# Final normalisation of the last block: three tiles' products moved from VectorE to ScalarE and GpSimd, the last tile worked in halves

## The chip, the cores and the metric

One core of a Trainium2 chip runs the whole program. The metric is the device time of one execution in microseconds (us), the median of several runs. TensorE multiplies matrices, VectorE (DVE), ScalarE (ACT) and GpSimd (POOL) work element by element, SyncE (SP) issues the transfers. The engines run their own instruction streams in the written order and meet only at semaphores.

## The reference

One step of a decoder layer over 1024 prompt rows and 64 sampled rows of 1024 columns: a matrix memory and a windowed attention, merged and projected, then an MLP with squared ReLU, and at the end a root-mean-square norm with learned weights. The change touches only that norm:

```python
def rmsnorm(x, g):
    y = x * lax.rsqrt(jnp.mean(x * x, axis=-1, keepdims=True) + EPS)
    return y * g

x = x + jnp.square(jax.nn.relu(xn2 @ w_up)) @ w_down
y_prompt, y_sample = rmsnorm(x_prompt_rows, norm_final), rmsnorm(x_sample_rows, norm_final)
```

## The kernel before

The 1088 rows are nine tiles of up to 128 rows (the ninth, tile 8, holds the 64 sampled rows), kept in `x2` in on-chip memory. The MLP's 4096 hidden columns are taken in 16 blocks of 256. Blocks 0 to 14 use a fast matrix scheme with seven half-size products; the last block is done plainly, tile by tile, in the order `DN_ORDER` = 8, 0, 4, 1, 5, 2, 6, 3, 7. Below, n is the place in that order (0 to 8) and not the tile's number, and d = 2n or 2n + 1 is a half tile of 512 columns.

For each half tile TensorE (`last_down`, L1362, products at L1385) makes a sum in one of six PSUM banks, used in turn: half tile d can start when half tile d - 6 has been read. VectorE (`accumulate`, L2390) adds the bank to `x2`. For n = 0 two parts of the sampled rows are first folded together (`fold`, L2396) after a small transfer inside the chip (L839).

Then comes the norm of each tile. ScalarE squares a tile and sums each row (`square`, L1428). GpSimd turns the sum into a rate per row, `rms`: a scaled addition (L2460), then a power of -1/2 (L2462), into `rstd`. VectorE multiplies the tile by rate and weights in one instruction (`normalise`, L1860; for the last tile two instructions of half a tile, L2422) into `ybuf`. SP stores `ybuf` to HBM (L843; the last tile in halves, L847).

`ybuf` has two slots, n % 2. A writer of a slot first waits until the store of tile n - 2 has landed (`y_out`). The weights `gain_b` are loaded at L837, once that buffer is no longer needed by the blocks before.

VectorE's written order is: accumulate 0, 1, 2, fold, final 0, then accumulate 3, final 1, final 2, accumulate 4, final 3, accumulate 5, final 4 and so on to accumulate 8, final 7, final 8. ScalarE's order is the nine squares, GpSimd's the nine rates, SP's the stores by n. Each waits for its inputs' semaphores, and nothing passes what stands ahead of it in its own stream.

Of the kernel before, what the change touches and what calls it, by code (L numbers as in the profile page):

```python
# [32 lines left out]
ALU = mybir.AluOpType  # L33
ACT = mybir.ActivationFunctionType

P = 128
D = 1024
# [4 lines left out]
NT = (T + P - 1) // P  # L42
# [10 lines left out]
EPS = 1e-6  # L53
# [20 lines left out]
def rows_of(i):  # L74
    return P if i < NT - 1 else T - P * (NT - 1)
# [36 lines left out]
MASKW = WIN + (2 * NSEQ - 1) * DSEQ  # L112
UP_UNITS = 2 * len(CHUNKS)
LAST_UNITS = 2 * NT
DN_ORDER = [NT - 1, 0, 4, 1, 5, 2, 6, 3, 7]
NS = NSEQ * DSEQ
FIRST_ORDER = [(0, 0), (0, 1), (0, 2), (1, 1), (1, 2), (1, 0)]
# [4 lines left out]
LAST = NG - 1  # L122
# [12 lines left out]
def up_unit_of(g, u):  # L135

    return (FIRST_ORDER if isinstance(g, int) and g == 0 else UP_ORDER)[u]


def unit_bank(g, u):  # L140

    return (0, 1, 2, 3, 6, 7)[u] if isinstance(g, int) and g == 0 else (6, 7, 0, 1, 2, 3)[u]
# [19 lines left out]
def tile_of(t):  # L162

    return t % NT if t < 2 * NT else DN_ORDER[t % NT]

# [87 lines left out]
def layer_kernel(nc, x_prompt, x_sample, state_C, state_n, state_m, cache_k, cache_v, norm_attn, w_in, b_gate,  # L253
# [9 lines left out]
    def y_rows(i):  # L263
        return y_prompt[0, i * P:(i + 1) * P, :] if i < NT - 1 else ys_flat
# [9 lines left out]
    with ctx:  # L274
# [7 lines left out]
        def sem(name):  # L282
            return ctx.enter_context(nc.semaphore(name))
# [9 lines left out]
        gain_b = sb("gain_b", [P, D])  # L293
# [6 lines left out]
        stat = sb("stat", [P, 3, NT])  # L300
        rstd = sb("rstd", [P, 3, NT])
        neghalf = sb("neghalf", [P, 2])
# [4 lines left out]
        with ExitStack() as s:  # L307
            a = scope_alloc(s)
            x2 = a("x2", [P, NT, D])
# [9 lines left out]
            with ExitStack() as s2:  # L319
                a2 = scope_alloc(s2)  # L320
                ybuf = a2("ybuf", [P, 2, D])
                junk2 = a2("junk2", [P, D])
# [92 lines left out]
        gain_in = sem("gain_in")  # L415
        const_in = sem("const_in")
        consts = sem("consts")
        norm_sq = sem("norm_sq")
        norm_rs = sem("norm_rs")
# [7 lines left out]
        free_v = sem("free_v")  # L427
# [91 lines left out]
        y_out = [sem(f"y_out{n}") for n in range(2)]  # L519
        folded = sem("folded")  # L520
        folded_in = sem("folded_in")
        y_rdy = sem("y_rdy")
        out_dma = sem("out_dma")


# [66 lines left out]
        def read(g, n):  # L592

            return g * DN_READS + (OUT_UNITS + n)
# [12 lines left out]
        def _(sp):  # L607
# [231 lines left out]
            sp.dma_start(hf[0:NS, 0, 0:D], x2[NS:P, NT - 1, :]).then_inc(folded, 16)  # L839
            *sooner, i = DN_ORDER  # L840
            for n, t in enumerate(sooner):
                sp.wait_ge(y_rdy, n + 1)
                sp.dma_start(y_rows(t), ybuf[0:rows_of(t), n % 2, :]).then_inc(y_out[n % 2], 16)  # L843
            for half in range(2):
                at = slice(half * 512, half * 512 + 512)
                sp.wait_ge(y_rdy, NT + half)
                sp.dma_start(y_rows(i)[:, at], ybuf[:, (NT - 1) % 2, at]).then_inc(y_out[(NT - 1) % 2], 16)  # L847
            sp.wait_ge(pc_out, 64)
            sp.wait_ge(cin_out[0], 2 * 16 * PAIRS)
# [6 lines left out]
        def _(pe):  # L856
# [505 lines left out]
            def last_down():  # L1362
# [3 lines left out]
                pe.wait_ge(lo_done, g * UP_UNITS + 4)  # L1366
                for n, i in enumerate(DN_ORDER):
                    if n == 1:
# [39 lines left out]
        def _(act):  # L1408
# [15 lines left out]
            def square(t, src, to):  # L1424
                rows = rows_of(tile_of(t))
                if t:
                    act.wait_ge(norm_sq, t)
                ins = nc.scalar.activation(to[0:rows, :], src, ACT.Square,  # L1428
                                           accum_out=stat[0:rows, t // NT, t % NT:t % NT + 1])
                ins.then_inc(norm_sq, 1)  # L1430
# [318 lines left out]
            for i in range(NT):  # L1749
                t = NT + i  # L1750
# [8 lines left out]
            def split_hid(g, u):  # L1759

                tile, parts, m = hid_parts(g, u)
                c0 = CHUNKS[up_unit_of(g, u)[1]][0]
                for to, at, n in parts:
                    ins = nc.scalar.activation(a_hi[:, to:to + n], relu[:, u % 2, at - c0:at - c0 + n], ACT.Square)
                if m:
                    ins = nc.scalar.activation(smp[:, tile, 0:m], relu[:, u % 2, SEQ - c0:SEQ - c0 + m], ACT.Square)
                ins.then_inc(hi_done, 1)
# [6 lines left out]
            def read_up(g):  # L1774

                sums = not isinstance(g, int) or g < LAST
                for u in range(UP_UNITS):
                    cn = CHUNKS[up_unit_of(g, u)[1]][1]
                    act.wait_ge(gemm_a, g * UP_UNITS + (PROJ_UNITS + u + 1))
                    if u >= 2 or not isinstance(g, int) or g:  # L1780
                        act.wait_ge(lo_done, g * UP_UNITS + (u - 1))
                    nc.scalar.activation(relu[:, u % 2, 0:cn], bank[unit_bank(g, u)][:, 0:cn],  # L1782
                                         ACT.Relu).then_inc(free_a, 1)
                    act.wait_ge(free_a, g * UP_UNITS + (PROJ_UNITS + u + 1))
                    split_hid(g, u)
                    if u == 1:
                        split_mlp(g * 16 + (RAW_ALL[1] + 16), 1)
                    if u == 2 and sums:
                        act.wait_ge(t_f, g * 4 + 4)
                        nc.scalar.activation(t_hi[:, :], tf[:, :], ACT.Copy).then_inc(t_h, 1)  # L1790
                    if u == (3 if not isinstance(g, int) or g else 4) and sums:
                        round_sum(g, S1)
                    if u == 4 and sums:
                        round_sum(g, S2)
                        round_sum(g, S3)
# [26 lines left out]
            with act.Fori(1, LAST) as g:  # L1822
                read_up(g)
                read_down(g)
            read_up(LAST)
            for n, i in enumerate(DN_ORDER):
                if i == NT - 1:
                    act.wait_ge(folded_in, 1)
                else:
                    act.wait_ge(free_v, read(LAST, 2 * n + 2))  # L1830
                square(2 * NT + n, x2[0:rows_of(i), i, :], junk2)

        @block.vector
        def _(dve):
# [345 lines left out]
            at = part_cols(0, 0)  # L2180
# [4 lines left out]
            at = part_cols(0, 1)  # L2185
# [44 lines left out]
            for cq in range(4):  # L2230
                for i in range(NT):
# [9 lines left out]
                    v = x2[0:r, i, cq // 2 * 512:cq // 2 * 512 + 512]  # L2241
                    ins = nc.vector.tensor_tensor(v, bank[m % out_ring(m)][0:r, :], v, ALU.add)
                    if i == NT - 1:
                        link(ins)
                        ins = nc.vector.tensor_tensor(v, bank[m % out_ring(m)][NS:P, :], v, ALU.add)
# [136 lines left out]
            def accumulate(n):  # L2382
                i = DN_ORDER[n]
                for half in range(2):
                    d = 2 * n + half
                    dve.wait_ge(gemm_v, LAST * DN_UNITS + OUT_UNITS + d + 1)
                    v = half_of(i, half)
                    if i < HB:
                        dve.wait_ge(halves, HB * half + i + 1)
                    nc.vector.tensor_tensor(v, bank[LAST_BANKS[d % len(LAST_BANKS)]][:, :], v, ALU.add).then_inc(free_v, 1)  # L2390
# [18 lines left out]
            def final(n):  # L2409
                i = DN_ORDER[n]  # L2410

                def slot():
                    if n >= 2:
                        dve.wait_ge(y_out[n % 2], 16 * (n // 2))
                if n < NT - 1:
                    normalise(2 * NT + n, x2[0:rows_of(i), i, :], ybuf, slot).then_inc(y_rdy, 1)
                    return
                dve.wait_ge(norm_rs, 3 * NT)
                slot()
                for half in range(2):  # L2420
                    at = slice(half * 512, half * 512 + 512)
                    nc.vector.scalar_tensor_tensor(ybuf[:, n % 2, at], x2[:, i, at], rstd[:, 2, n:n + 1], gain_b[:, at],  # L2422
                                                   ALU.mult, ALU.mult).then_inc(y_rdy, 1)

            accumulate(0)
            accumulate(1)
            accumulate(2)
            fold()
            for n in range(2, NT):
                if n > 2:  # L2430
                    accumulate(n)
                if n <= 3:
                    final(n - 2)
                if n >= 3:
                    final(n - 1)
            final(NT - 1)

# [1 line left out]
        def _(pool):  # L2439
            chain = [0]  # L2440

            def link(ins):

                chain[0] += 1
                ins.then_inc(pool_chain, 1)
                pool.wait_ge(pool_chain, chain[0])
# [9 lines left out]
            def rms(t):  # L2456
                rows = rows_of(tile_of(t))
                pool.wait_ge(norm_sq, t + 1)
                v = rstd[0:rows, t // NT, t % NT:t % NT + 1]
                link(nc.gpsimd.tensor_scalar(v, stat[0:rows, t // NT, t % NT:t % NT + 1], 1.0 / D, EPS,  # L2460
                                             ALU.mult, ALU.add))
                nc.gpsimd.tensor_tensor(v, v, neghalf[0:rows, 0:1], ALU.pow).then_inc(norm_rs, 1)  # L2462
# [140 lines left out]
            for q in range(HB):  # L2603
                v = x2[:, q, 0:HD2]
# [3 lines left out]
            for q in range(HB):  # L2608
                lo = x2[:, q, HD2:D]
                nc.gpsimd.tensor_tensor(lo, lo, e6[:, q, :], ALU.add).then_inc(halves, 1)  # L2610
            for t in range(2 * NT, 3 * NT):
                rms(t)


_INS = ["x_prompt", "x_sample", "state_C", "state_n", "state_m", "cache_k", "cache_v", "norm_attn", "w_in", "b_gate",
# [23 lines left out]
```

## Time and profile before

| | us |
|---|---|
| median of 3 runs (lowest, highest) | 1666.8 (1664.81, 1667.55) |
| the profiled execution | 1666.46 |
| its span, first to last instruction | 1664.7 |
| TensorE busy in the span | 1638.7 (98%) |
| VectorE busy | 949.5 (57%) |
| ScalarE busy | 633.2 (38%) |
| GpSimd busy | 349.5 (21%) |

The span is that of the profiled execution; its device time has 1.76 us more around it. The mean granted TensorE clock over the span was 0.996 of full speed. Over the whole span TensorE is the busy engine; the change lies in the last 30 us, from about 1634 us on. TensorE's last product starts at 1654.17 us.

### The profile page before, as it was taken

The numbers are of one execution on the slowest core, as the hardware profiler recorded it, in microseconds if no ns is written. First come the engines' busy times: TensorE is split into PE (matmuls) and PEld (weight loads), VectorE is DVE, ScalarE is ACT, GpSimd is POOL, SyncE is SP. The second block draws the span as 40 slices with busy tenths as digits, with TensorE's granted clock in tenths as the row PEclk, the third lists the DMA queues.
The fourth block names the chain that finished last, engine by engine and source line by source line (L and its number), as shares of the span: only waits on it lengthen the run. The fifth ranks groups of instructions, "written<-read, shape, count | busy, mean of one in ns | idle before, by whom it ended". The sixth has DMA issues, their size and how long they took to land.

```text
span 1664.7 us, 26791 instructions
## 1 busy us (share of the span) xinstructions
PE 1638.7 (98%) x10035; PEld 1496.3 (90%) x10035; DVE 949.5 (57%) x1753; ACT 633.2 (38%) x1407; POOL 349.5 (21%) x351
## 2 busy tenths in 40 slices
PE   8999999999999999999999999999999999999997
PEld 8999899899998899888988899999999999999996
DVE  5413333343145445774545877667777777767787
ACT  5523333232235423553402533433344443343332
POOL 2002001110002100111001233333333222333354
PEclk9999999999999999999999999999999999999999
DMA  7105355352311132311241101111111111111113
GB/s 219 53 26 137 61 73 100 51 88 29 69 29 27 28 82 46 61 27 26 64 134 50 48 29 51 50 50 50 50 33 43 50 50 50 50 38 38 50 63 114
DMA packets 138793, 99.46 MB, mean 60 GB/s; under 512 B 82376, under 2 KB 128464, under 8 KB 138712
## 3 DMA queue, kind: packets, MB, share of 16 engines
q1 hardware_dynamic: 138712, 98.34, 23.8%
q8 instruction: 55, 0.90, 0.2%
q14 instruction: 26, 0.21, 0.0%
HBM read 88.43 MB, written 11.60 MB: 60 GB/s over the span
## 4 chain that ended last, share of the span: by engine, by line
PE 96%; DVE 2%; ACT 1%; issue 1%; DMA 1%; another core or an unknown queue 0%; SPq 0%; POOL 0%; DVEq 0%; POOLq 0%; ACTq 0%
PE bank L911 37%; PE bank L1276 23%; PE bank L1309 6%; PE bank L1310 6%; PE bank L1308 6%; PE bank L1256 5%; PE bank L858 3%; PE bank L1317 2%; PE bank L1097 2%; PE bank L1067 1%; PE bank L976 1%; PE bank L968 1%; PE bank L971 1%; PE bank L1014 1%; PE bank L951 0%
## 5 line engine op out<-in xcount | busy, mean ns | idle before, releaser
L1276 PE MATMUL bank<-xT_hi,w_hi 128*128 128x384 f32 (+1 forms) x768 | 250.7, 326 | 1.0 <-DVE xT_lo L1875 1.0
L1276 PE MATMUL bank<-xT_hi,w_lo 128*128 128x384 f32 (+1 forms) x768 | 250.6, 326 | 0.0
L1276 PE MATMUL bank<-xT_lo,w_hi 128*128 128x384 f32 (+1 forms) x768 | 250.5, 326 | 0.0
L911 PE MATMUL bank<-xT_hi,w_hi 128*128 128x384 f32 (+1 forms) x1008 | 193.9, 334 | 0.0
L911 PE MATMUL bank<-xT_hi,w_lo 128*128 128x384 f32 (+1 forms) x1008 | 186.2, 326 | 0.0
L911 PE MATMUL bank<-xT_lo,w_hi 128*128 128x384 f32 (+1 forms) x1008 | 186.1, 326 | 0.0
L2578 POOL TENSOR_TENSOR e<-gain_b,e 128x512 f32<-128x512 f32 x60 | 78.2, 1304 | 435.0 <-ACT gain_b L1804 435.0
L911 PEld LDWEIGHTS bank<-xT_hi,w_hi 128*128 128x128 f32 x1008 | 166.7, 188 | 2.7 <-issue 1.3
L911 PEld LDWEIGHTS bank<-xT_lo,w_hi 128*128 128x128 f32 x1008 | 168.7, 188 | 0.0
L911 PEld LDWEIGHTS bank<-xT_hi,w_lo 128*128 128x128 f32 x1008 | 168.7, 188 | 0.0
L2358 DVE TENSOR_TENSOR x<-bank,x 128x512 f32<-128x512 f32 x210 | 142.0, 690 | 31.5 <-PE bank L1310 30.9
L1850 DVE TENSOR_TENSOR w_lo<-raw,w_hi 128x1024 fp32r<-128x1024 f32 (+1 forms) x54 | 70.4, 1303 | 155.8 <-ACT w_hi L1421 155.8
L1276 PEld LDWEIGHTS bank<-xT_hi,w_hi 128*128 128x128 f32 x768 | 144.1, 188 | 1.8 <-DVE xT_lo L1875 1.2
L1276 PEld LDWEIGHTS bank<-xT_lo,w_hi 128*128 128x128 f32 x768 | 144.2, 188 | 0.6
L1276 PEld LDWEIGHTS bank<-xT_hi,w_lo 128*128 128x128 f32 x768 | 144.1, 188 | 0.0
L1804 ACT ACTIVATE gain_b<-bank 128x512 f32<-128x512 f32 x120 | 71.8, 599 | 147.2 <-PE bank L1310 82.7
L2298 DVE TENSOR_TENSOR hf<-relu 128x384 f32<-128x384 f32 (+1 forms) x96 | 55.8, 582 | 114.2 <-ACT relu L1782 114.1
L1782 ACT ACTIVATE relu<-bank 128x384 f32<-128x384 f32 (+1 forms) x96 | 45.2, 471 | 197.8 <-PE bank L1276 195.9
L1500 ACT ACTIVATE sig<-bank 128x384 f32<-128x384 f32 (+1 forms) x72 | 34.1, 474 | 173.8 <-PE bank L911 173.8
L1308 PE MATMUL bank<-t_hi,a_hi 128*128 128x512 f32 x240 | 93.4, 389 | 1.3 <-issue 1.3
L1309 PE MATMUL bank<-t_hi,a_lo 128*128 128x512 f32 x240 | 94.2, 393 | 0.0
L1310 PE MATMUL bank<-t_lo,a_hi 128*128 128x512 f32 x240 | 94.1, 392 | 0.0
(275 smaller groups left out, 3009.5 us busy)
## 6 DMA issues: line engine op xcount, KB each, us to landing
raw<-in_w_in SPq DMA_DIRECT2D x64, 256.0 KB, 4.5
raw<-in_w_up SPq DMA_DIRECT2D x16, 1024.0 KB, 5.3
raw<-in_w_down SPq DMA_DIRECT2D x16, 1024.0 KB, 5.0
raw<-in_w_in SPq DMA_DIRECT2D x9, 1024.0 KB, 5.6
xin<-in_x_prompt SPq DMA_DIRECT2D x8, 512.0 KB, 4.0
bc<-gate_rows SPq DMA_DIRECT2D x32, 128.0 KB, 5.7
Cin<-in_state_C SPq DMA_DIRECT2D x4, 1024.0 KB, 8.1
out<-Cin SPq DMA_DIRECT2D x16, 256.0 KB
```

The lines of the kernel that those rows point to most:

```text
L858: return nc.tensor.transpose(out, in_, ident[0:rows, 0:rows])
L911: last = nc.tensor.matmul(out, lhsT, rhs, start=(step == 0), stop=(step == 3 * KT - 1))
L1256: last = nc.tensor.matmul(bank[m % out_ring(m)][0:rows_of(i), :], lhsT, w[:, b % 2, g * 512:(g + 1) * 512], start=(step == 0), stop=(step ...
L1276: last = nc.tensor.matmul(bank[unit_bank(g, u)][:, 0:cn], w[:, 0, k * WCOLS + tile * P:k * WCOLS + (tile + 1) * P], x[:, k, c0:c0 + cn], s ...
L1308: nc.tensor.matmul(out[:, :], a_tile(a_hi, a, q), b_part(b, False), start=True, stop=False)
L1309: nc.tensor.matmul(out[:, :], a_tile(a_lo, a, q), b_part(b, False), start=False, stop=False)
L1310: nc.tensor.matmul(out[:, :], a_tile(a_hi, a, q), b_part(b, True), start=False, stop=True).then_inc(gemm_v, 1)
L1804: nc.scalar.activation(gain_b[:, at:at + HD2], bank[PLACE.index(name) % BANKS][:, :], ACT.Copy).then_inc(free_c, 1)
L1850: ins = nc.vector.tensor_tensor(w_lo[:, b % 2, at], raw[:, b % 2, at], w_hi[:, b % 2, at].bitcast(F32), ALU.subtract)
L2298: nc.vector.tensor_tensor(hf[:, tile, c0:c0 + cn], relu[:, u % 2, 0:cn], relu[:, u % 2, 0:cn], ALU.mult).then_inc(sq_done, 1)
L2358: nc.vector.tensor_tensor(v, src, v, ALU.add).then_inc(free_v, 1)
L2578: nc.gpsimd.tensor_tensor(v, gain_b[:, at:at + HD2], v, ALU.add).then_inc(c_added, 1)
```

## The change

At three places of the order, n = 1, 3, 5 (`Y_POOL`), the final product is no longer one VectorE instruction. ScalarE scales the tile by its row rates into `ybuf` (`scale_row`, in ScalarE's stream behind the square of n + 1, and behind the wait for the slot), and GpSimd multiplies that slot in place by the weights (`scaled_by_gain`, in GpSimd's stream behind the rate of n + 1). SP waits for GpSimd's semaphore `y_pool` for these tiles; its order of stores stays.

For the last tile, ScalarE squares each half of 512 columns as soon as that half is accumulated, into two sums; GpSimd joins them in an added instruction. VectorE multiplies the second half by the weights without the rate, then, when the rate is there, does the first half's whole product as before; ScalarE scales the second half. SP stores the first half after VectorE's product, the second after ScalarE's scaling.

VectorE's order becomes: accumulate 0, 1, 2, fold, final 0, accumulate 3, final 2, accumulate 4, accumulate 5, final 4, accumulate 6, accumulate 7, final 6, accumulate 8, final 7, final 8.

```diff
+Y_POOL = (1, 3, 5)
...
             for n, t in enumerate(sooner):
-                sp.wait_ge(y_rdy, n + 1)
+                if n in Y_POOL:
+                    sp.wait_ge(y_pool, Y_POOL.index(n) + 1)
+                else:
+                    sp.wait_ge(y_rdy, n + 1 - sum(x < n for x in Y_POOL))
                 sp.dma_start(y_rows(t), ybuf[0:rows_of(t), n % 2, :]).then_inc(y_out[n % 2], 16)
             for half in range(2):
                 at = slice(half * 512, half * 512 + 512)
-                sp.wait_ge(y_rdy, NT + half)
+                if half:
+                    sp.wait_ge(y_last, 1)
+                else:
+                    sp.wait_ge(y_rdy, NT - len(Y_POOL))
...
+            def scale_row(n):
+
+                i = DN_ORDER[n]
+                act.wait_ge(norm_rs, 2 * NT + n + 1)
+                if n >= 2:
+                    act.wait_ge(y_out[n % 2], 16 * (n // 2))
+                nc.scalar.activation(ybuf[:, n % 2, :], x2[:, i, :], ACT.Copy,
+                                     scale=rstd[:, 2, n:n + 1]).then_inc(y_scaled, 1)
+
             for n, i in enumerate(DN_ORDER):
                 if i == NT - 1:
                     act.wait_ge(folded_in, 1)
-                else:
+                elif n < NT - 1:
                     act.wait_ge(free_v, read(LAST, 2 * n + 2))
-                square(2 * NT + n, x2[0:rows_of(i), i, :], junk2)
+                if n < NT - 1:
+                    square(2 * NT + n, x2[0:rows_of(i), i, :], junk2)
+                if n - 1 in Y_POOL:
+                    scale_row(n - 1)
+            act.wait_ge(norm_sq, 3 * NT - 1)
+            for half in range(2):
+                at = slice(half * 512, half * 512 + 512)
+                act.wait_ge(free_v, read(LAST, 2 * NT - 1 + half))
+                ins = nc.scalar.activation(junk2[:, at], x2[:, DN_ORDER[-1], at], ACT.Square,
+                                           accum_out=stat[:, 2 * half, NT - 1:NT])
+                ins.then_inc(norm_sq if half else sq_half, 1)
+            act.wait_ge(norm_rs, 3 * NT)
+            act.wait_ge(y_gained, 1)
+            nc.scalar.activation(ybuf[:, (NT - 1) % 2, 512:D], ybuf[:, (NT - 1) % 2, 512:D], ACT.Copy,
+                                 scale=rstd[:, 2, NT - 1:NT]).then_inc(y_last, 1)
...
+                slot()
+                dve.wait_ge(free_v, read(LAST, 2 * NT))
+                nc.vector.tensor_tensor(ybuf[:, n % 2, 512:D], x2[:, i, 512:D], gain_b[:, 512:D],
+                                        ALU.mult).then_inc(y_gained, 1)
                 dve.wait_ge(norm_rs, 3 * NT)
-                slot()
-                for half in range(2):
-                    at = slice(half * 512, half * 512 + 512)
-                    nc.vector.scalar_tensor_tensor(ybuf[:, n % 2, at], x2[:, i, at], rstd[:, 2, n:n + 1], gain_b[:, at],
-                                                   ALU.mult, ALU.mult).then_inc(y_rdy, 1)
+                nc.vector.scalar_tensor_tensor(ybuf[:, n % 2, 0:512], x2[:, i, 0:512], rstd[:, 2, n:n + 1],
+                                               gain_b[:, 0:512], ALU.mult, ALU.mult).then_inc(y_rdy, 1)
...
-            for n in range(2, NT):
-                if n > 2:
-                    accumulate(n)
-                if n <= 3:
-                    final(n - 2)
-                if n >= 3:
+            final(0)
+            for n in range(3, NT):
+                accumulate(n)
+                if n - 1 not in Y_POOL:
                     final(n - 1)
             final(NT - 1)
...
-            for t in range(2 * NT, 3 * NT):
-                rms(t)
+            def scaled_by_gain(n):
+
+                pool.wait_ge(y_scaled, Y_POOL.index(n) + 1)
+                v = ybuf[:, n % 2, :]
+                nc.gpsimd.tensor_tensor(v, v, gain_b[:, :], ALU.mult).then_inc(y_pool, 1)
+
+            pool.wait_ge(gain_in, 48)
+            for n in range(NT - 1):
+                rms(2 * NT + n)
+                if n - 1 in Y_POOL:
+                    scaled_by_gain(n - 1)
+            v = rstd[:, 2, NT - 1:NT]
+            pool.wait_ge(sq_half, 1)
+            link(nc.gpsimd.tensor_scalar(v, stat[:, 0, NT - 1:NT], 1.0 / D, EPS, ALU.mult, ALU.add))
+            pool.wait_ge(norm_sq, 3 * NT)
+            link(nc.gpsimd.tensor_scalar(v, stat[:, 2, NT - 1:NT], 1.0 / D, v, ALU.mult, ALU.add))
+            nc.gpsimd.tensor_tensor(v, v, neghalf[:, 0:1], ALU.pow).then_inc(norm_rs, 1)
```

## Rows read from the trace of the kernel before

**Rows 1.** Busy us by stretch (start:end, length, engines with instruction counts, clock, DMA).

```profile
1643.40:1654.90 11.50, 11.17 (x48) 8.63 (x47) 10.82 (x14) 4.86 (x10) 5.88 (x10) 1.00 0.55 207
1654.90:1664.70 9.80, 0.00 (x0) 0.00 (x0) 6.28 (x9) 2.37 (x5) 2.23 (x6) 0.74 0.53 214
```

**Rows 2.** Timeline of VectorE (start us, us, engine, line, operation, count [idle before]).

```profile
1642.18 1.27 DVE L1860 SCALAR_TENSOR_TENSOR ybuf<-x,rstd,gain_b 64x1024 f32<-64x1024 f32 x1 [2.12 <-POOL rstd L2462]
1643.38 1.27 DVE L2390 TENSOR_TENSOR x<-bank,x 128x512 f32<-128x512 f32 x2
1644.58 1.27 DVE L1860 SCALAR_TENSOR_TENSOR ybuf<-x,rstd,gain_b 128x1024 f32<-128x1024 f32 x1
1646.52 1.28 DVE L1860 SCALAR_TENSOR_TENSOR ybuf<-x,rstd,gain_b 128x1024 f32<-128x1024 f32 x1 [0.68 <-DMA out<-ybuf]
...
1658.49 1.28 DVE L1860 SCALAR_TENSOR_TENSOR ybuf<-x,rstd,gain_b 128x1024 f32<-128x1024 f32 x1
1660.70 1.41 DVE L2422 SCALAR_TENSOR_TENSOR ybuf<-x,rstd,gain_b 128x512 f32<-128x512 f32 x2 [0.94 <-POOL rstd L2462]
```

**Rows 3.** Timeline of TensorE: first and last product of the last block.

```profile
1631.90 0.50 PE L1385 MATMUL bank<-w_hi,a_hi 128*128 128x512 f32 x1
...
1654.17 0.40 PE L1385 MATMUL bank<-w_lo,a_hi 128*128 128x512 f32 x1
```

**Rows 4.** Timeline of SyncE's queue: the stores, and the second half's store.

```profile
1643.48 16.65 SPq L843 DMA_DIRECT2D out<-ybuf  x8
...
1662.14 0.33 SPq L847 DMA_DIRECT2D out<-ybuf  x1
```

**Rows 5.** DMA issues at 1643.48, at 1650.23, and from 1655: count, size, us to landing.

```profile
out<-ybuf SPq DMA_DIRECT2D x1, 256.0 KB, 3.0
...
out<-ybuf SPq DMA_DIRECT2D x1, 512.0 KB, 3.3
...
out<-ybuf SPq DMA_DIRECT2D x3, 512.0 KB, 2.6
out<-ybuf SPq DMA_DIRECT2D x2, 256.0 KB, 2.0
```

**Rows 6.** Timeline of GpSimd: rates per row.

```profile
1643.59 0.55 POOL L2462 TENSOR_TENSOR rstd<-rstd,neghalf 128x1 f32<-128x1 f32 x1
1644.23 0.19 POOL L2460 TENSOR_SCALAR rstd<-stat 128x1 f32<-128x1 f32 x1
1644.50 1.76 POOL L2462 TENSOR_TENSOR rstd<-rstd,neghalf 128x1 f32<-128x1 f32 x1
...
1646.62 1.59 POOL L2462 TENSOR_TENSOR rstd<-rstd,neghalf 128x1 f32<-128x1 f32 x1
```

**Rows 7.** Lines 2578 and 2584 of GpSimd: duration ns min/median/max, first and last start.

```profile
L2578 POOL TENSOR_TENSOR x<-gain_b,x x60: 1277/1302/1347, 970.2 to 1604.8; 128x512 f32<-128x512 f32 x60
...
L2584 POOL TENSOR_TENSOR w_lo<-raw,w_hi x15: 4617/4621/4632, 965.7 to 1596.5; 128x2048 fp32r<-128x2048 f32 x15
```

**Rows 8.** Timelines of VectorE and GpSimd near 937 us, at 1630.66 and 1601 to 1607 us.

```profile
936.99 4.29 DVE L2298 TENSOR_TENSOR hf<-relu 128x384 f32<-128x384 f32 x1
...
936.25 4.62 POOL L2598 TENSOR_TENSOR x<-x 128x2048 f32<-128x2048 f32 x1 [5.16 <-issue]
...
1630.66 0.56 DVE L2298 TENSOR_TENSOR hf<-relu 128x384 f32<-128x384 f32 x1 [0.78 <-ACT relu L1782]
...
1602.89 4.18 DVE L2358 TENSOR_TENSOR x<-bank,x 128x512 f32<-128x512 f32 x6 [0.70 <-PE bank L1310]
...
1601.06 5.04 POOL L2578 TENSOR_TENSOR x<-gain_b,x 128x512 f32<-128x512 f32 x4
```

**Rows 9.** Timeline of ScalarE: one square and its row sums.

```profile
1642.58 1.06 ACT L1428 ACTIVATE junk<-x 128x1024 f32<-128x1024 f32 x1
1643.54 0.19 ACT L1428 ACTIVATION_READ_ACCUMULATOR junk<-x 128x1 f32 x1
```

**Rows 10.** Line 1747 of ScalarE: duration ns min/median/max, first and last start.

```profile
L1747 ACT ACTIVATE w_hi<-raw x32: 1901/1905/1916, 906.9 to 1615.0; 128x2048 fp32r<-128x2048 f32 x32
```

More of the change, by code:

```diff
@@ L522, in layer_kernel @@
         y_rdy = sem("y_rdy")
+        y_scaled = sem("y_scaled")
+        y_pool = sem("y_pool")
+        y_gained = sem("y_gained")
+        y_last = sem("y_last")
+        sq_half = sem("sq_half")
         out_dma = sem("out_dma")
```

## The prediction

> **What bounds the kernel now.** Read first the busy time by stretch [rows 1]. While TensorE still works on the last block (1643.40 to 1654.90), VectorE is busy 10.82 of 11.50 us; after TensorE's end it is still busy 6.28 of 9.80 us. Then VectorE's own order of time [rows 2]: from 1643.38 on it alternates two accumulates (1.27 us a tile, 1.20 to the next) with one final product (1.28 us, 1.20 to the next), 2.40 us a tile. TensorE's product instructions [rows 3] start at 1631.90 and 1654.17, 95 steps for 16 half tiles of six, so 1.407 us a half tile and 2.81 a tile, and the last sum is ready at 1654.17 + 0.40 = 1654.57. VectorE is faster per tile but began late; its last accumulates end as the last whole product begins, about 1658.5. The last 6.1 us are a chain: square, reciprocal root, product in two halves, stores issued one behind the other, the second at 1662.14, and the span ends 2.56 us later [rows 4]. The VectorE wait at 1646.52 (0.68 us, ended by a store [rows 2]) is the one to notice: ybuf has two slots, and a slot is free only when its store has landed. The 256 KB store of tile n = 0, issued at 1643.48, landed 3.0 us later; whole tiles take 2.6 to 3.3 us [rows 5]. Elsewhere a slot comes round every 4.8 us (two tiles) and nobody waits.
>
> **What is removed.** Three final products leave VectorE: 3 x 1.20 = 3.6 us. The last tile's square (1.06 us plus 0.19 for its sum [rows 9]) is halved so that one half runs ahead of the last accumulate, about 0.5 us; its two half products (1.41 us [rows 2]) run side by side on two engines, about 0.65 us. VectorE gets a separate gain product of half a tile in exchange, 0.70 us by half of that 1.41, beside the square. GpSimd gets one small extra step, 0.19 + 0.08 us as its others [rows 6], under the second half square. All of this pays only if VectorE's work sets the end.
>
> **What is added: a ring.** Tiles n = 1, 3, 5 use slot 1 of ybuf, every one of them; n = 7 does too, on VectorE. For each, ScalarE scales by the row rate, GpSimd multiplies by the weights in place, SP stores, and only then may ScalarE write the slot for the next. Costs of one turn:
> - ScalarE, 128x1024: no row with a rate per row. Nearest is the square of the same shape, 1.06 us [rows 9]; half of the 2048-column copy, 0.95 us [rows 10], is the bound below, square with its sum, 1.25, the one above. I take 1.06.
> - GpSimd product, 128x1024: rows at 512 columns (1.30 us) and 2048 (4.62 us) [rows 7]. The line through them gives 2.4 us; bounds are half of the long one, 2.31, and two short ones, 2.60. I take 2.40.
> - Store to landing 2.6 us, up to 3.3 [rows 5]; I take 2.6.
> - Three handoffs, 0.03 to 0.05 us each as between engines in the rows: 0.13.
>
> A turn is 1.06 + 2.40 + 2.60 + 0.13 = 6.19 us against 4.8 before. n = 1 can start when its rate is there, 1643.59 + 0.55 [rows 6], so 1644.18.
>
> Of the store the Trainium skill (DMA: Bandwidth & Descriptors, "Anatomy of one DMA — SWDGE (gpsimd) path") gives a fit for GpSimd's own DMAs, a fixed 2.0 us and then the bytes at 436 GB/s; an estimate for 512 KB by that page is 3.2 us. The stores of this tail, issued by SP, took 2.0 us for 256 KB and 2.6 for 512 KB [rows 5], which leaves 1.4 fixed. By the page two of the landings on the chain would each be 0.6 longer and the sum below 1.2 us higher; I go by the rows.
>
> **Engines that block each other.** GpSimd's root, 0.55 us alone, took 1.76 and 1.59 us where it began at 1644.50 and 1646.62 [rows 6], beside VectorE's products of 1644.58 and 1646.52 [rows 2]: it ended only after they did. The other way round, a VectorE subtraction that takes 0.56 us elsewhere took 4.29 us beside a GpSimd instruction of 4.62 us, and ended just after it [rows 8]. So one holds the other off for a whole instruction. A GpSimd product of 2.40 us now falls among VectorE's products. Six additions of VectorE that read a bank, as the accumulates do, took 0.70 us each from 1602.89, beside four GpSimd additions of 1.26 us [rows 8]: neither was stretched, and I charge accumulates nothing.
>
> **The sum, step by step.** Scale n = 1: 1644.18 to 1645.24. GpSimd product 1645.29 to 1647.69; its store lands 1650.3. VectorE, after accumulate 3, wants product n = 2 at 1646.52 but is held to 1647.69 and passes on at 1648.89; accumulate 4 ends 1650.16 (before: 1648.9). TensorE's half tile d = 14 is due at 1631.90 + 12 x 1.407 = 1648.8 and needs the first bank of accumulate 4, so it loses about 0.7 us; this is covered, VectorE reads that bank later anyway. ScalarE's square 4 ends 1651.33, and only behind it comes scale 3: ScalarE works in its written order. Scale 3 ends 1652.39; VectorE's product n = 4 started at 1652.24 (rate ready) and holds GpSimd off to 1653.50. GpSimd product 1653.50 to 1655.90, store issued 1655.93, landed 1658.53. SP issues in order, so the finished tile n = 4 is stored behind it, at 1656.28, landing about 1659.0. Scale 5: 1658.58 to 1659.64. VectorE's product n = 6 has waited for the n = 4 landing and runs about 1659.1 to 1660.4; accumulate 8 stands behind it. GpSimd product 1660.4 to 1662.8, store landed 1665.43. VectorE's product n = 7 wants that slot: 1665.48, next instruction at +1.20, gain product +0.60, last half product +0.75: 1668.03. Stores at 1668.05 and 1668.40. End 2.56 us later: 1670.96 against 1664.7, so +6.3 us.
> Both gains of the last tile, the halved square and the shared product, are hidden: its rate is ready near 1664.6, ahead of 1668. If n = 7 did not wait, they would be worth the 0.5 and 0.65 us above.
>
> The profiled execution took 1666.46 us, 1.76 around its span, 0.3 below the median of 1666.8. 1666.46 + 6.3 = 1672.8; against the median 1673.1. I take 1673.0.
>
> **Rivals.**
> - **It works as the load suggests: faster.** The mechanism is VectorE relieved: it keeps up with TensorE, accumulate 8 ends 0.7 us after 1654.57, half square 0.75 (half of 1.06, 0.19, a handoff), GpSimd 0.95 (0.19 and 0.55 with handoffs), half product 0.8, second store issue 0.4, end 2.56: 1660.7, so 1662.5 us. For it: 10.82 of 11.50 us busy [rows 1]. The Trainium skill (Perfetto Trace Analysis, "Optimizing Scalar/DVE Operations") says the same, that a saturated VectorE may be relieved by the other two, with the warning that GpSimd shares a port with it; the trace agrees that VectorE is the busy one. Against: the ring. From n = 7's start to the second last-tile store issue are 2.92 us; to keep 1662.14 it must start by 1659.2, which wants a turn of 5.0 us or less. The rows give 6.2. Chance 6%.
> - **No holding off between whole products.** Then the ring alone counts: 1644.18 + 3 x 6.19 = 1662.75, n = 7 at 1662.8, second store 1665.7, end 1668.3, +3.6 us: 1670.0. Against it: [rows 6, 8]. Chance 13%.
> - **A longer ring.** Landings of 3.3 us add 0.7 for each of two stores; 2.60 us products add 0.2 each; at 1659.6 the order of GpSimd's product and VectorE's n = 6 is close, and if GpSimd goes first accumulate 8 and the last square slip behind it. Together up to +8.5: 1675.0. Chance 11%.
>
> **Chances.** Forecast 70%, its own range 1671.5 to 1674.5 (order at 1659.6 swapped, prices of the ring within their bounds, and the spread of the runs shown). 13%, 11%, 6% for the rivals. The range from the second rival to the third, 1669.8 to 1675.3, leaves out mainly the first. 0.2% (3.3 us) is about what a measurement of this kernel can tell from no change. Slower by more: the forecast, the third rival and most of the rest of the margin of the second, which sits at that bound: 70 + 11 + 6 = 87%. Same: 7%. Faster: 6%.
>
> **What would show it.** Right: GpSimd products of about 2.4 us, the first ending near 1647.7 and two later ones ending only after a VectorE product; VectorE idle, ended by a store, ahead of n = 6 and for some 4 us ahead of n = 7; accumulate 8 near 1660 to 1662 although its sums were ready 5 us sooner; little wait for the last rate. Wrong: stores issued every 2.4 us to the end, GpSimd products under 1.5 us, or accumulate 8 right behind TensorE's last product. A landing near 2.0 us or a store issued before the product is done in my order would shorten the ring and break the sum.

## The result, and the profile after

| | median us | runs | ratio to the kernel before |
|---|---|---|---|
| before | 1666.0 | 6 | |
| changed | 1672.42 (1671.06 to 1675.22) | 6 | 1.0041, interval 1.0031 to 1.0051 |

The changed kernel is slower by 0.41% (6.4 us); the forecast was 1673.0, which is 6.2 us over the 1666.8 known then. The profiled execution took 1671.98 us, its span is 1670.3.

First the same stretches of the busy time as before, and the one that was added at the end. The columns are the start and end, the length, then PE, PEld, DVE, ACT and POOL busy with their instruction counts, clock and DMA.

```profile
1643.40:1654.90 11.50, 10.10 (x43) 7.49 (x41) 8.43 (x10) 6.08 (x10) 8.73 (x9) 1.00 0.33 115
1654.90:1664.70 9.80, 0.00 (x0) 0.00 (x0) 5.63 (x4) 3.52 (x7) 5.93 (x8) 0.73 0.53 214
1664.70:1670.30 5.60, 0.00 (x0) 0.00 (x0) 1.58 (x3) 0.72 (x1) 1.43 (x2) 0.50 0.47 187
```

Against [rows 1] VectorE is busy 8.43 us in the first stretch in place of 10.82, GpSimd 8.73 in place of 5.88: the load moved as written. But no engine is near full after TensorE's end, and the stretch lasts longer. The end is waiting, so the next view is who waited for whom (the whole tail from 1641 us; total, times, longest).

```profile
DVE ybuf L1895 <- DMA out<-ybuf: 6.3, 3, 4.0
...
DVE ybuf L1895 <- POOL rstd L2496: 3.1, 2, 2.2
...
ACT ybuf L1844 <- DMA out<-ybuf: 2.7, 1, 2.7
...
PEld bank L1397 <- DVE x L2425: 1.1, 1, 1.1
```

VectorE's waits for stores went from 0.7 us (its one such wait in [rows 2]) to 6.3, and ScalarE waits for a store too. TensorE, which before waited for VectorE only at the first load of this block (0.4 us), loses 1.1 us at the weight load that follows accumulate 4's late read. The order of time of TensorE (first and last product), VectorE, ScalarE and GpSimd shows where:

```profile
1630.57 0.49 PE L1397 MATMUL bank<-w_hi,a_hi 128*128 128x512 f32 x1
...
1653.75 0.40 PE L1397 MATMUL bank<-w_lo,a_hi 128*128 128x512 f32 x1
```

```profile
1645.27 2.36 DVE L1895 SCALAR_TENSOR_TENSOR ybuf<-x,rstd,gain_b 128x1024 f32<-128x1024 f32 x1 [1.88 <-DMA out<-ybuf]
1647.55 2.47 DVE L2425 TENSOR_TENSOR x<-bank,x 128x512 f32<-128x512 f32 x4
1650.95 1.28 DVE L1895 SCALAR_TENSOR_TENSOR ybuf<-x,rstd,gain_b 128x1024 f32<-128x1024 f32 x1 [0.93 <-POOL rstd L2496]
1652.15 2.48 DVE L2425 TENSOR_TENSOR x<-bank,x 128x512 f32<-128x512 f32 x4
1658.58 3.36 DVE L1895 SCALAR_TENSOR_TENSOR ybuf<-x,rstd,gain_b 128x1024 f32<-128x1024 f32 x1 [3.96 <-DMA out<-ybuf]
1661.87 1.27 DVE L2425 TENSOR_TENSOR x<-bank,x 128x512 f32<-128x512 f32 x2
1663.63 1.28 DVE L1895 SCALAR_TENSOR_TENSOR ybuf<-x,rstd,gain_b 128x1024 f32<-128x1024 f32 x1 [0.49 <-DMA out<-ybuf]
1664.84 0.69 DVE L2455 TENSOR_TENSOR ybuf<-x,gain_b 128x512 f32<-128x512 f32 x1
1666.25 0.75 DVE L2458 SCALAR_TENSOR_TENSOR ybuf<-x,rstd,gain_b 128x512 f32<-128x512 f32 x1 [0.72 <-POOL rstd L2661]
```

```profile
1642.91 1.15 ACT L1844 ACTIVATE ybuf<-x,rstd 128x1024 f32<-128x1024 f32 x1 [0.52 <-POOL rstd L2496]
...
1657.30 1.15 ACT L1844 ACTIVATE ybuf<-x,rstd 128x1024 f32<-128x1024 f32 x1 [2.68 <-DMA out<-ybuf]
```

```profile
1644.14 2.40 POOL L2649 TENSOR_TENSOR ybuf<-ybuf,gain_b 128x1024 f32<-128x1024 f32 x1 [0.35 <-ACT ybuf L1844]
...
1651.13 3.39 POOL L2649 TENSOR_TENSOR ybuf<-ybuf,gain_b 128x1024 f32<-128x1024 f32 x1 [0.21 <-ACT ybuf L1844]
...
1658.52 2.34 POOL L2649 TENSOR_TENSOR ybuf<-ybuf,gain_b 128x1024 f32<-128x1024 f32 x1 [2.20 <-ACT ybuf L1844]
...
1664.15 1.44 POOL L2660 TENSOR_SCALAR rstd<-stat,rstd 128x1 f32<-128x1 f32 x1 [0.51 <-ACT junk L1860]
```

TensorE's products of the last block at L1397 (L1385 before) began at 1630.57 here and at 1631.90 in [rows 3]: the profiled executions differ by 1.33 us before the change is reached. So the profiles are compared below by the tail, from the first of these products to the end of the span: 1664.7 - 1631.90 = 32.80 us before, 1670.3 - 1630.57 = 39.73 us after, +6.93. Each tail is that of one execution.

Two readings. GpSimd's product takes 2.40 us where it began first (1644.14), and VectorE's product of 1645.27 is stretched beside it from 1.28 to 2.36: it ends 1.1 us after GpSimd's. At 1651.13 it is the other way: VectorE's product began at 1650.95, and GpSimd's takes 3.39. And accumulate 8 (1661.87) starts 7.7 us after TensorE's last product, because VectorE's product of n = 6 stands ahead of it and waited 3.96 us for a store and then for GpSimd.

The chain of work that ended last, as the profile follows it back (start, length, what), runs from the store of n = 4 through that product, accumulate 8 and the last rate, and not through the wait for n = 7's slot, which is 0.49 us. GpSimd's joining step of the last rate (1664.15) ends only behind product 7 and the gain product, so those 0.49 us may count in it:

```profile
1654.91 3.57 DMA out<-ybuf
...
1658.58 3.36 DVE ybuf L1895
1661.94 0.61 DVE x L2425
...
1662.64 1.34 ACT junk L1860 x4
...
1664.15 1.44 POOL rstd L2660
...
1666.25 0.75 DVE ybuf L2458
```

### The profile page after: what moved, and what is told of

Same layout as the page of the kernel before. It is cut to its first block, busy times and chain, and to the rows that moved or that the text cites. A ratio compares the mean times of both kernels' runs of the same rounds, so it can differ in the third digit from the quotient of the medians.

```text
span 1670.3 us, 26801 instructions
## 1 busy us (share of the span) xinstructions
PE 1639.0 (98%) x10035; PEld 1496.2 (90%) x10035; DVE 949.1 (57%) x1750; ACT 637.2 (38%) x1413; POOL 357.8 (21%) x355
## 4 chain that ended last, share of the span: by engine, by line
PE 96%; DVE 2%; ACT 1%; DMA 1%; issue 1%; POOL 0%; SPq 0%; POOLq 0%; DVEq 0%; ACTq 0%
PE bank L923 36%; PE bank L1288 23%; PE bank L1321 6%; PE bank L1322 6%; PE bank L1320 6%; PE bank L1268 5%; PE bank L870 3%; PE bank L1329 2%; PE bank L1109 2%; PE bank L1079 1%; PE bank L988 1%; PE bank L980 1%; PE bank L983 1%; PE bank L1026 1%; PE bank L963 0%
```

## The experiments

Each run is given as its ratio to the kernel before, run on the same chip, and as the tail of its profile (32.80 us before, 39.73 changed). Medians of the kernel before were 1664.68 us for the first four, 1665.2 for the next four, 1665.31 for the last, against 1666.0 above, so the expectations' absolute times are to be read from the kernel before of the same chip.

| run | median us (kernel before) | ratio, 95% interval | tail us |
|---|---|---|---|
| e1 own places | 1667.5 (1664.68) | 1.0019, 1.001 to 1.0028 | 35.21 |
| e3 three tiles only | 1671.13 (1664.68) | 1.004, 1.0026 to 1.0054 | 39.11 |
| e4 fills for products | 1669.3 (1664.68) | 1.0033, 1.0021 to 1.0046 | 37.02 |
| e5 no products | 1665.73 (1664.68) | 1.0006, 0.9997 to 1.0016 | 33.40 |
| e2 last tile only | 1666.13 (1665.2) | 1.0007, 0.9998 to 1.0016 | 33.32 |
| e6 products in halves | 1673.05 (1665.2) | 1.0051, 1.0038 to 1.0065 | 40.79 |
| e7 order, own places, halves | 1665.02 (1665.2) | 0.9998, 0.9989 to 1.0007 | 31.93 |
| e8 own places, no products | 1664.11 (1665.2) | 0.9995, 0.9986 to 1.0004 | 31.63 |
| e9 order, own places | 1663.15 (1665.31) | 0.9989, 0.998 to 0.9998 | 31.28 |

**e1: the ring taken away.** Every tile's result goes to a place of its own, in buffers that are dead by then, and the waits for stores go:

```diff
+        def y_slot(n):
+            spare = (None, None, e1, e1, e5, e5, e6, e6)
+            if n < 2:
+                return ybuf[:, n, :]
+            if n == NT - 1:
+                return hf[:, 1, 0:D]
+            return spare[n][:, n % 2 * 2:n % 2 * 2 + 2, :].rearrange("p a c -> p (a c)")
...
-                if n >= 2:
-                    act.wait_ge(y_out[n % 2], 16 * (n // 2))
```

Expected: 

> The changed kernel with a place of its own for every tile's result, so that no engine waits for a store; the GpSimd products, the queue orders and the last tile's halves stay. Theory (the ring of two slots sets the end): about 5 us come back, near 1667 us, with a rest of about 1 us over the kernel before, because GpSimd's rates still stand behind its products and products still hold each other off. Rival (the slow GpSimd product and the engines holding each other off cost the time by themselves): at most 2 us come back, 1670 us or more.

Measured: 2.8 us over the kernel before, tail 35.21. Of the 6.9 us of the tail 4.5 came back, of the 6.4 us of the medians 3.6: nearer to the theory's 5 than to the rival's 2 at most. The rest is above what was expected, and VectorE's waits (total, times, longest; `e` is one of the new places) and GpSimd's first product say what it is:

```profile
DVE e L2457 <- POOL rstd L2502: 5.9, 4, 2.0
```

```profile
1643.56 3.24 POOL L2655 TENSOR_TENSOR ybuf<-ybuf,gain_b 128x1024 f32<-128x1024 f32 x1 [0.35 <-ACT ybuf L1851]
```

VectorE now waits 5.9 us for rates, more than the 3.6 us that it was spared. GpSimd makes the rates, and the products, 3.24, 3.24 and 3.18 us long in this trace, stand ahead of them in its stream. Three products of 2.40 would be 7.20 us; the other 2.46 are holding off by VectorE's products. The chain that ended last in e1 runs through all three.

**e4: the same turn, nothing read.** Two fills of dead memory in place of each product; the weights of three tiles are left out.

```diff
-                nc.gpsimd.tensor_tensor(v, v, gain_b[:, :], ALU.mult).then_inc(y_pool, 1)
+                nc.gpsimd.memset(e1[:, :, :], 0.0)
+                nc.gpsimd.memset(e6[:, 0, :], 0.0).then_inc(y_pool, 1)
```

Expected: 

> The changed kernel with each GpSimd product replaced by two fills of other, dead memory that together take about the same 2.4 us; it leaves out the weights of three tiles. The ring keeps its turn, but GpSimd reads nothing. If GpSimd's reads are what holds VectorE off, the VectorE products of n = 2 and n = 6 fall back to 1.28 us, and the end comes to the ring alone: 1669 to 1670.5 us. Rival (holding off is of no weight in the end, the ring's turn is all): within 0.7 us of the changed kernel. If fills hold VectorE off as well, its products stay stretched and the time stays.

Measured: 4.6 us over the kernel before, tail 37.02, 2.7 under the changed kernel's. GpSimd and VectorE beside each other, and VectorE's product of n = 7:

```profile
1643.43 1.81 POOL L2648 MEMSET e<- 128x2048 f32 x1 [0.33 <-ACT ybuf L1844]
1645.18 0.53 POOL L2649 MEMSET e<- 128x512 f32 x1
```

```profile
1644.57 1.28 DVE L1895 SCALAR_TENSOR_TENSOR ybuf<-x,rstd,gain_b 128x1024 f32<-128x1024 f32 x1 [1.87 <-DMA out<-ybuf]
...
1661.01 1.28 DVE L1895 SCALAR_TENSOR_TENSOR ybuf<-x,rstd,gain_b 128x1024 f32<-128x1024 f32 x1 [2.47 <-DMA out<-ybuf]
```

Neither is stretched, here or at the other two places. The fills took 2.28 us together, 0.12 less than a product, so a turn is nearly the same: from each scaling to the next write of the slot 6.30, 6.25 and 6.24 us in this trace, against 6.19 in the prediction, and n = 7 waits 2.47 us for its slot. The ring without holding off, the halved last tile with it, costs 4.2 us of tail (the second rival of the prediction had 3.6). The engines' holding each other off is worth most of the other 2.7 us, by these two profiles; by the medians the difference is 1.8 us, and the intervals of the two ratios overlap. The Trainium skill (SBUF — State Buffer, "Who interferes with whom") says that a VectorE instruction with two SBUF inputs contends with a GpSimd instruction that reads SBUF and not with one that only writes it; the trace agrees, 1.28 us beside the fill against 2.36 beside the product.

**e6: the product in two halves**, so that VectorE can come between.

```diff
-                v = ybuf[:, n % 2, :]
-                nc.gpsimd.tensor_tensor(v, v, gain_b[:, :], ALU.mult).then_inc(y_pool, 1)
+                for at in (slice(0, 512), slice(512, D)):
+                    v = ybuf[:, n % 2, at]
+                    ins = nc.gpsimd.tensor_tensor(v, v, gain_b[:, at], ALU.mult)
+                ins.then_inc(y_pool, 1)
```

Expected: 

> The changed kernel with each GpSimd product cut into two instructions of half a tile (1.3 us each), so that VectorE's product can come between. If the ring sets the end: VectorE's products of n = 2 and 6 are stretched less, but GpSimd's second half, and with it the store and the next turn, comes later where they meet; the end moves little or is up to 2 us later than the changed kernel (kernel before + 6 to + 8). Rival (it costs because VectorE is held off for a whole GpSimd product): 1 us or more earlier than the changed kernel, kernel before + 5 or less.

Measured: 7.9 us over the kernel before, tail 40.79. VectorE's products of n = 2 and n = 6, and GpSimd's two halves beside them:

```profile
1644.70 1.28 DVE L1895 SCALAR_TENSOR_TENSOR ybuf<-x,rstd,gain_b 128x1024 f32<-128x1024 f32 x1 [1.88 <-DMA out<-ybuf]
...
1658.73 2.29 DVE L1895 SCALAR_TENSOR_TENSOR ybuf<-x,rstd,gain_b 128x1024 f32<-128x1024 f32 x1 [2.79 <-DMA out<-ybuf]
```

```profile
1643.58 3.56 POOL L2650 TENSOR_TENSOR ybuf<-ybuf,gain_b 128x512 f32<-128x512 f32 x2 [0.35 <-ACT ybuf L1844]
...
1658.66 3.47 POOL L2650 TENSOR_TENSOR ybuf<-ybuf,gain_b 128x512 f32<-128x512 f32 x2 [1.83 <-ACT ybuf L1844]
```

At n = 2 VectorE is no longer stretched; at n = 4 and 6 it still is (2.32 and 2.29 us). In all its products are stretched by 2.05 us in place of 3.16, while GpSimd's take 10.53 us in place of 8.13. The tail is 1.1 us longer; by the timings alone e6 is not told from the changed kernel. Less holding of VectorE, a longer turn and no time won: the rival, which wanted 1 us or more less, falls. Part of the longer turn is the cut itself, two halves of 1.30 us for one product of 2.40.

**e5 and e8: no products at all.** ScalarE's scaled tile is stored at once; the weights of three tiles are left out. e8 has own places as well.

```diff
-                                     scale=rstd[:, 2, n:n + 1]).then_inc(y_scaled, 1)
+                                     scale=rstd[:, 2, n:n + 1]).then_inc(y_pool, 1)
...
-                if n - 1 in Y_POOL:
-                    scaled_by_gain(n - 1)
```

Expected of e5: 

> The changed kernel without the GpSimd products: ScalarE's scaled tile is stored at once; it leaves out the weights of three tiles. A turn of the ring falls to 1.15 + 2.6 + 0.1 = 3.9 us, under the 4.8 of the kernel before. Theory (the GpSimd product in the ring is what costs): VectorE's relief shows, 1662 to 1664.5 us. Rival (the order in ScalarE's and SP's queues is what costs): 1666 us or more.

Expected of e8: 

> The changed kernel without the GpSimd products and with a place of its own for every tile; it leaves out the weights of three tiles. Neither a store nor a GpSimd product can hold anything up, so what is left over the kernel before, or gained, is VectorE's relief of 3.6 us against the waits for rates. Theory (with the store waits gone too, part of the relief shows): 1 to 3 us under the kernel before. Rival (the waits for rates in the written order take all of it): within 0.8 us of the kernel before.

Measured: e5 1.1 us over the kernel before, not resolved from it, tail 33.40; e8 1.1 us under, not resolved either, tail 31.63. The products cost 6.3 us of tail in the ring (39.73 to 33.40) and 3.6 outside it (35.21 of e1 to 31.63); the ring costs 4.5 with the products and 1.8 without. The two feed each other, and neither has a price of its own. And e5's theory missed: VectorE's relief of 3.6 us does not show. Its waits in e5:

```profile
DVE ybuf L1895 <- POOL rstd L2496: 4.1, 3, 2.2
DVE ybuf L1895 <- DMA out<-ybuf: 2.2, 2, 1.9
```

One of these, 2.2 us, is the wait for the first rate that stands in [rows 2] too. The others are new: in the written order the product of n = 2 comes right behind accumulate 3 and waits 1.9 us for the store of n = 0, those of n = 4 and 6 come right behind two accumulates and wait 0.9 us each for a rate. In e8 the store waits are gone, three rates are still waited for (2.3 us), and 1.2 us of tail are gained, of 3.6; the timings leave e8's rival, within 0.8 us of the kernel before, standing.

**e3 and e2: the two parts of the change by themselves.** e3 keeps the three tiles and does the last tile as before; e2 is `Y_POOL = ()` with product 1 on VectorE again, and keeps the last tile's halves.

Expected of e3: 

> The changed kernel with only the three moved products; the last tile is done as before (one square, two VectorE half products). Theory (the end waits for the ring, so the last tile's halves buy next to nothing): within 0.7 us of the changed kernel, 1672 to 1673 us. Rival (the halves save their 1.1 us and the three tiles cost that much more): 1 us or more above the changed kernel.

Expected of e2: 

> The change to the last tile alone: all whole products on VectorE in the order of the kernel before, the last square in halves, the last product on two engines. If the halves are worth what they were costed at when nothing waits for a slot, 1.1 us under the kernel before. Rival, from the trace of the changed kernel (GpSimd's joined sum waits for VectorE's product of n = 7 and for the added gain product, both of which hold it off): within 0.6 us of the kernel before, rather above it than below.

Measured: e3 6.45 us over the kernel before, tail 39.11, 0.6 less than with the halves; up to product 7 its trace and that of the changed kernel agree within 0.02 us, counted from the tail's start. e2 0.9 us over, not resolved from the kernel before, tail 33.32, 0.5 more than before. So nearly the whole cost is the three tiles', and the halves save nothing in either run; by the profiles they cost about half a us, which the timings can't separate from nothing. VectorE and GpSimd at the end of e2:

```profile
1661.44 1.27 DVE L1895 SCALAR_TENSOR_TENSOR ybuf<-x,rstd,gain_b 128x1024 f32<-128x1024 f32 x1
1662.99 0.69 DVE L2455 TENSOR_TENSOR ybuf<-x,gain_b 128x512 f32<-128x512 f32 x1 [0.28 <-DMA out<-ybuf]
1664.12 0.75 DVE L2458 SCALAR_TENSOR_TENSOR ybuf<-x,rstd,gain_b 128x512 f32<-128x512 f32 x1 [0.44 <-POOL rstd L2663]
```

```profile
1661.83 0.94 POOL L2660 TENSOR_SCALAR rstd<-stat 128x1 f32<-128x1 f32 x1 [0.60 <-ACT junk L1860]
...
1663.22 0.87 POOL L2663 TENSOR_TENSOR rstd<-rstd,neghalf 128x1 f32<-128x1 f32 x1
```

The first half's sum is there early, but GpSimd's 0.19 us step takes 0.94, until VectorE's product of n = 7 is done, and its root takes 0.87 in place of 0.55 beside the added gain product.

**e7 and e9: the version that the runs point to.** Own places, no moved product, and VectorE's accumulates ahead of products whose rate or place is not ready; e7 with the last tile in halves, e9 with the last tile as before.

```diff
             accumulate(0)
             accumulate(1)
             accumulate(2)
             fold()
-            for n in range(2, NT):
...
+            accumulate(3)
+            final(0)
+            accumulate(4)
+            final(1)
+            final(2)
+            accumulate(5)
+            final(3)
...
+            accumulate(8)
+            final(6)
+            final(7)
+            final(8)
```

Expected of e7: 

> No GpSimd or ScalarE product for n = 1, 3, 5; every tile has a place of its own; VectorE's accumulates stand ahead of products whose rate is not ready (accumulate 3 before product 0, accumulate 4 before product 1, and so on to accumulate 8 before product 6); last tile in halves. If waits in VectorE's written order are what keeps the tail long, accumulate 8 follows TensorE's last product within 1.2 us and the end is 1.5 to 2.5 us under the kernel before. Rival (after accumulate 8 the products of n = 6 and 7 and the last rate stand one behind the other as they did): within 0.8 us of the kernel before.

Expected of e9: 

> The kernel before with two things changed: a place of its own for every tile's result and VectorE's accumulates ahead of products whose rate is not ready (accumulate 8 ahead of products 6 and 7); the last tile as before. If the added steps of the halved last tile (a gain product on VectorE, a joined sum on GpSimd that both wait for each other) cost about 0.5 us, as its trace shows, this is 0.5 us below the same order with halves: 0.7 to 1.7 us under the kernel before. Rival (halves pay once the tail is in this order): 0 to 0.5 us above the same order with halves, within 0.6 us of the kernel before.

Measured: e7 level with the kernel before, e9 faster than it by 0.11% (interval 0.02% to 0.20%), the only one of the runs above that is below it by more than its interval. That is 2.2 us by the medians and 1.5 by the tails, where 0.7 to 1.7 was expected; no run has the new order without own places, so the gain isn't split between the two. e7's expectation missed its gain though accumulate 8 came where it was expected, 0.2 us after TensorE's last product: GpSimd and VectorE after it in e7, then VectorE in e9.

```profile
1658.34 1.78 POOL L2675 TENSOR_SCALAR rstd<-stat,rstd 128x1 f32<-128x1 f32 x1
```

```profile
1656.92 2.46 DVE L2457 SCALAR_TENSOR_TENSOR e<-x,rstd,gain_b 128x1024 f32<-128x1024 f32 x2
1659.31 0.67 DVE L2461 TENSOR_TENSOR hf<-x,gain_b 128x512 f32<-128x512 f32 x1
```

```profile
1654.45 2.47 DVE L2442 SCALAR_TENSOR_TENSOR e<-x,rstd,gain_b 128x1024 f32<-128x1024 f32 x2
1657.65 1.41 DVE L2448 SCALAR_TENSOR_TENSOR hf<-x,rstd,gain_b 128x512 f32<-128x512 f32 x2 [0.72 <-POOL rstd L2495]
```

In e7 GpSimd's joining step, 0.27 us in e2's trace, takes 1.78 us behind VectorE's product of n = 7 and the gain product. In e9 VectorE has no gain product, the rate comes 0.72 us after product 7, and the tail is 0.65 us shorter than e7's.

## Why the prediction was right

Times of the changed kernel are given here plus 1.33 us, on the clock of the rows of before.

- **The ring.** Scale 1 at 1644.24 (predicted 1644.18), GpSimd's product 1645.47 to 1647.87 (1645.29 to 1647.69), scale 3 at 1651.24 (1651.33), its product held off by product 4 and ended at 1655.85 (1655.90), scale 5 at 1658.63 (1658.58). The prices were right: product 2.40 us (2.40 taken), scale 1.15 (1.06 taken, at most 1.25).
- **Engines that block each other.** Product 2 ended at 1648.96 (predicted 1648.89) and TensorE lost about 1 us behind accumulate 4 (0.7), covered as said. e4 puts a price on holding off, at most 2.7 us of tail (1.8 by the medians); the sum had 6.3 - 3.6 = 2.7. One reading behind it has a wrong name: the VectorE instruction of 4.29 us in [rows 8] is a multiplication, not a subtraction; its times stand.
- **A step that went the other way.** "GpSimd product 1660.4 to 1662.8", behind VectorE's product n = 6 at "about 1659.1": GpSimd was first, at 1658.52 against 1658.58 in the trace's own time. The prediction named this order as close. What decided it is a landing: the store of n = 4, issued 0.37 us behind that of n = 3, took 3.6 us where about 2.7 was reckoned. It moved accumulate 8 from 1660.4 to 1663.2 and product 7 only from 1665.5 to 1665.0. So the sign "for some 4 us ahead of n = 7" did not come: VectorE waited 0.49 us there, and the end hung on accumulate 8 and the last rate in the first place. By the sum's own last steps VectorE would have ended 0.5 us sooner than predicted; it ended 0.3 later. That the number holds to 0.7 us at the end is in part luck: the mechanism was right up to scale 5, the last links of the path were not.
- **The failed side remark.** "Its rate is ready near 1664.6, ahead of 1668", and both halves' gains "would be worth the 0.5 and 0.65 us" without the wait. The last rate was not ahead: it was ready at 1667.55, and VectorE waited 0.72 us for it. GpSimd's joining step had taken 1.44 us, behind VectorE's product 7 and the gain product (0.27 in e2's trace). e2 shows that the halves are worth nothing without the three products either, e7 beside e9 that by their tails own places don't change this. The step left out that GpSimd's small steps are held off by VectorE's products, though the prediction had read just that from the roots of [rows 6].
- **The faster rival's time** (1662.5 us) was too low. Its condition, a ring under 5.0 us a turn, is met in e5 and goes away in e8, and neither comes near: waits for rates and stores in the written order take the place of VectorE's work. Its sum had none of these waits.
- **The end.** Second store of the last tile at 1668.73 (predicted 1668.40). The tail grew by 6.93 us against 6.3 in the sum, by the median 6.4.

What stays open: how e1's remaining 2.4 us of tail split between the rates behind GpSimd's products and the holding off. Its trace has both on the chain that ended last, but no run has own places and fills.

## What to carry to other kernels

When a step moves from one engine to two others, add up the whole turn of its buffer (write, second write, store, landing) and compare it with the time in which the buffer came round before: here 6.2 us by the rows, 7.0, 7.4 and 6.3 in the trace of the changed kernel, against 4.8. The three GpSimd products spared VectorE 1.2 us each and stretched two of its other products by 1.1 and 2.1 us, so little of the relief was left, and small GpSimd steps on the last chain stand behind VectorE's products in turn. A busy engine's load is worth only what the next wait in its written order leaves: without the products and all ring waits, 3.6 us of relief left 1.2 us of tail, which the timings don't tell from nothing.

## What the runs showed of the hardware that was not expected

- ScalarE's scaling with a rate per row took 1.15 us where the square of the same shape takes 1.06. The Trainium skill (ScalarE: Activation LUTs, "What ACT_TABLE_LOAD costs") gives about 93 ns for each per-partition operand; the 0.09 us agree.
- A 512 KB store issued 0.37 us behind another landed after 3.6 us; the other six of that size in the changed kernel's tail after 2.6 to 2.9. The DMA issue at 1654.91 of the changed kernel (count, size, us to landing):

```profile
out<-ybuf SPq DMA_DIRECT2D x1, 512.0 KB, 3.6
```

- A waiting GpSimd step isn't always let in between two VectorE products: in e7 it stood behind two in a row (1.78 us for 0.27), and so it did in the changed kernel (1.44).
